# Gates of a PEER layer: tile 0's scattered by indirect DMAs into a table in HBM, tile 1's by one-hot products

## What is computed

```python
q = (xc @ wq).astype(F32).reshape(tc, H, 2, PEER_HALF)
s = jnp.einsum('thpd,hpnd->thpn', q, subkeys.astype(F32))
sv, si = lax.top_k(s, K)
cand = (sv[:, :, 0, :, None] + sv[:, :, 1, None, :]).reshape(tc, H, K * K)
cidx = (si[:, :, 0, :, None] * NK + si[:, :, 1, None, :]).reshape(tc, H, K * K)
best, pos = lax.top_k(cand, K)
eidx = jnp.take_along_axis(cidx, pos, axis=-1)
gates = jax.nn.softmax(best, axis=-1)
act = jax.nn.gelu(jnp.einsum('td,thkd->thk', xc, u_tab[eidx]).astype(F32), approximate=False)
w = (gates * act).astype(xc.dtype)
return jnp.einsum('thk,thkd->td', w, v_tab[eidx])
```

## Time and profile before

| what | value |
|---|---|
| median of 3 runs | 1063.74 us (1062.57 to 1065.11) |
| profiled execution | 1063.1 us |
| its span, first to last instruction | 1061.4 us |
| PE busy | 1039.0 us, 98% |
| DVE / ACT / POOL busy | 718.4 / 520.2 / 326.6 us |
| TensorE's granted clock, mean | 0.99 of full speed |
| moved by DMA | 205.43 MB, 194 GB/s on average |
| U's pieces of 512 KB | landing 3.7 us after issue |

### The profile page before, as it was taken

How to read it: one execution, slowest core, us unless ns; L and a number is a source line. 1 busy time by engine, 2 the same in 40 slices (tenths; PEclk the granted TensorE clock), 3 DMA queues, 4 the chain that set the end, 5 groups by cost and what they waited for, 6 DMA issues and landing times.

```text
span 1061.4 us, 18274 instructions
## 1 busy us (share of the span) xinstructions
PE 1039.0 (98%) x7154; PEld 963.8 (91%) x7154; DVE 718.4 (68%) x1601; ACT 520.2 (49%) x797; POOL 326.6 (31%) x161
## 2 busy tenths in 40 slices
PE   8999999889999999999999999999999999999996
PEld 8999889889999999999999999988888888888875
DVE  7778887964897069556666767765555756666556
ACT  5686657335444454544434343355544555455542
POOL 1000000001888788866666666600001000000002
PEclk9999999988999999999999999999999999999999
DMA  9878748544555555544444444456669567776651
GB/s 360 325 242 307 246 139 314 165 137 160 179 176 180 177 175 182 187 158 137 143 140 140 139 140 140 140 177 193 193 192 334 180 205 250 235 240 205 195 174 42
DMA packets 57413, 205.43 MB, mean 194 GB/s; under 512 B 6768, under 2 KB 8816, under 8 KB 56560
## 3 DMA queue, kind: packets, MB, share of 16 engines
q1 hardware_dynamic: 55616, 199.01, 57.0%
q0 software_dynamic: 1424, 5.24, 1.3%
q10 hardware_dynamic: 288, 0.01, 0.0%
HBM read 202.15 MB, written 2.10 MB: 192 GB/s over the span
## 4 chain that ended last, share of the span: by engine, by line
PE 91%; DVE 4%; ACT 1%; issue 1%; DMA 1%; SPq 0%; ACTq 0%; DVEq 0%
PE px L1079 33%; PE pw L786 16%; PE pw L787 16%; PE pw L788 15%; PE px L1051 5%; DMA ada<-in_ada 1%; DVE w_lo L1130 1%; PE px L1017 1%; PE px L786 1%; PE px L787 0%; PE px L788 0%; PE px L850 0%; ACT w_hi L487 0%; PE px L947 0%; PE pw L1099 0%
## 5 line engine op out<-in xcount | busy, mean ns | idle before, releaser
L487 ACT ACTIVATE w_hi<-raw 128x1024 fp32r<-128x1024 f32 x312 | 328.5, 1056 | 334.0 <-PE px L1079 168.8
L786 PE MATMUL pw<-a_hi,w_hi 128*128 128x256 f32 x1280 | 370.0, 289 | 2.1 <-DVE a_lo L1391 2.1
L787 PE MATMUL pw<-a_lo,w_hi 128*128 128x256 f32 x1280 | 362.6, 283 | 0.0
L788 PE MATMUL pw<-a_hi,w_lo 128*128 128x256 f32 x1280 | 362.5, 283 | 0.0
L420 POOL TENSOR_TENSOR w_lo<-raw,w_hi 128x1024 fp32r<-128x1024 f32 x128 | 307.5, 2403 | 142.2 <-ACT w_hi L487 140.9
L1130 DVE TENSOR_TENSOR w_lo<-raw,w_hi 128x1024 fp32r<-128x1024 f32 x184 | 224.5, 1229 | 156.0 <-ACT w_hi L487 155.3
L786 PEld LDWEIGHTS pw<-a_hi,w_hi 128*128 128x128 f32 x1280 | 245.8, 192 | 3.8 <-DVE a_lo L1391 2.5
L787 PEld LDWEIGHTS pw<-a_lo,w_hi 128*128 128x128 f32 x1280 | 246.1, 192 | 0.1
L788 PEld LDWEIGHTS pw<-a_hi,w_lo 128*128 128x128 f32 x1280 | 245.8, 192 | 0.0
L1079 PE MATMUL px<-w_hi,ws_hi 128*128 128x512 f32 x512 | 159.3, 390 | 0.9 <-DVE ws_lo L1543 0.9
L1079 PE MATMUL px<-w_lo,ws_hi 128*128 128x512 f32 x512 | 159.0, 389 | 0.0
(11 more groups left out here) (328 smaller groups left out, 1118.0 us busy)
## 6 DMA issues: line engine op xcount, KB each, us to landing
raw<-in_u SPq DMA_DIRECT2D x128, 512.0 KB, 3.7
raw<-in_v SPq DMA_DIRECT2D x128, 512.0 KB, 4.6
raw<-in_ws SPq DMA_DIRECT2D x56, 512.0 KB, 4.9
ada<-in_w_ada SPq DMA_DIRECT2D x32, 512.0 KB, 7.1
ada<-in_ada SPq DMA_DIRECT2D x6, 1024.0 KB, 11.1
raw<-in_w SPq DMA_DIRECT2D x7, 768.0 KB, 11.2
ada<-in_ada SPq DMA_DIRECT2D x4, 512.0 KB, 7.0
xT<-in_xT SPq DMA_DIRECT2D x8, 128.0 KB, 10.4
```

Source lines behind the costliest of these rows:

```text
L487: return nc.scalar.activation(out, in_, ACT.Copy, **kw)
L786: nc.tensor.matmul(out, lh, rh, start=start and x == 0, stop=False)
L787: nc.tensor.matmul(out, lh, rl, start=False, stop=False)
L788: last = nc.tensor.matmul(out, ll, rh, start=False, stop=stop and x == len(pairs) - 1)
```

## The change

Tile 0's gates no longer pass through one-hot products. A table of 128 x 128 x 128 floats in HBM (`gates_d`, 8.4 MB, laid out as j, i, token) is cleared, each gate of tile 0 is added into its place by indirect DMAs, and in V's stage each row's 64 KB are loaded back and multiplied into W's columns of tile 0. In detail:

- POOL clears the table by 8 DMAs of 1 MB from a zero tile of 256 floats per partition, one after every third of its splits. It now makes w_lo for U's first 26 pieces only, and DVE for the other 102.
- POOL then waits for the clears and for tile 0's gates, and issues 128 indirect DMAs (8 heads x 16 places), each with one word per partition and an add at its destination; before each further head it waits for all that it issued.
- DVE's top-k turns are cut into six steps. Tile 0's run in a row; tile 1's have a split before each step. `normal(0)` stands between the splits of U's pieces 27 and 28, and `normal(1)` at piece 74. The comparisons of both halves are one instruction each.
- The one-hot groups are 32, for tile 1's tokens from the last to the first, and come after the pieces 82 + 11n/8. iota is read from SBUF.
- SP waits, ahead of V's first piece, for the whole scatter and for the last one-hot matrices, then loads four rows of gates; from row 4 on, each load of V has one of gates behind it.
- DVE has a product `gate_w(r)` per V row, and ACT's `split_w` waits for it. ACT waits for the scatter at g = 63, since places and gates of tile 0 lie in W's last rows.

The diff, cut to its core:

```diff
-GA_U = 31
-OH = T // 4
-SCORES_AFTER = (4, 8, 11, 15)
-ENDS_AFTER = (18, GA_U - 2)
+SCORES_AFTER = (4, 8, 11, 14)
+POOL_PIECES = 26
+EXP_AFTER = (12, 36)
+NORMAL_AT = 74
+INDEX_AFTER = 38
+OH = P // 4
+OH_AT = [82 + 11 * n // 8 for n in range(OH)]
+GA_U = OH_AT[0] // 2
+ZERO = 256
+ZERO_DMAS = 8
...
+            def load_gates(r):
+
+                if r >= RING:
+                    sp.wait_ge(w_gated, r - RING + 1)
+                sp.dma_start(g_row[:, r % RING], gates_d[r * P * P:(r + 1) * P * P].rearrange("(i t) o -> i (t o)", i=P)) \
+                    .then_inc(g_landed[r % RING], 16)
+
             for m in range(UP, VP + NK):
+                if m == VP:
+                    sp.wait_ge(scattered, 16 * PH * TOPK)
+                    sp.wait_ge(oh_ready, OH)
+                    for r in range(RING):
+                        load_gates(r)
                 load_piece(m)
                 r = m - VP
+                if r >= RING:
+                    load_gates(r)
...
+            def clear(n):
+
+                pool.dma_start(table[n].rearrange("i (a f) -> i a f", f=ZERO),
+                               zero[:, :].unsqueeze(1).broadcast_to([P, NK * P // ZERO // ZERO_DMAS, ZERO])) \
+                    .then_inc(zero_landed, 16)
...
-            for m in range(UP, VP):
+            pool.wait_ge(zero_ready, 1)
+            for m in range(UP, UP + POOL_PIECES):
                 split_lo(m)
-
+                if (m - UP) % 3 == 2 and (m - UP) // 3 < ZERO_DMAS:
+                    clear((m - UP) // 3)
+
+            pool.wait_ge(zero_landed, 16 * ZERO_DMAS)
+            pool.wait_ge(gate_ready, 1)
+            for h in range(PH):
+                if h:
+                    pool.wait_ge(scattered, 16 * TOPK * h)
+                for k in range(TOPK):
+                    nc.gpsimd.indirect_dma_start(gates_d, bass.IndirectOffsetOnAxis(ap=place[:, h, k:k + 1], axis=0),
+                                                 gate[0][:, h, k:k + 1], None, compute_op=ALU.add).then_inc(scattered, 16)
...
             def split_w(v):
 
+                act.wait_ge(w_gated, v + 1)
...
+            for g in range(NG):
+                if g == 8:
+                    act.wait_ge(x1_spilled, 16)
                 if g == NG - 1:
-                    act.wait_ge(g_lower_taken, OH)
-                    for v in range(RING):
-                        split_w(v)
+                    act.wait_ge(scattered, 16 * PH * TOPK)
+                    for r in range(RING):
+                        split_w(r)
...
+            steps = (upper_half, lower_half, candidates, best_eight, next_eight, names)
...
+            for i in range(PH):
+                for step in steps:
+                    step(i)
+            gates(0)
+            upper_half(PH)
+            lower_half(PH)
+            dve.wait_ge(lo_ready, UP + POOL_PIECES)
+            m = UP + POOL_PIECES
+            for i in range(PH, TT * PH):
+                for n, step in enumerate(steps):
+                    split_lo(m)
+                    m += 1
+                    if i == PH and step is names:
+                        dve.wait_ge(zero_landed, 16 * ZERO_DMAS)
+                    if i > PH or n > 1:
+                        step(i)
+                    if i == PH and n == 1:
+                        normal(0)
+            gates(1)
+
+            def gate_w(r):
+
+                dve.wait_ge(g_landed[r % RING], 16 * (r // RING + 1))
+                dve.wait_ge(u_out, r // 2 + 1)
+                v.tensor_tensor(W[:, r, 0:P], W[:, r, 0:P], g_row[:, r % RING], ALU.mult).then_inc(w_gated, 1)
...
+            for p in range(m - UP - 3, 2 * NG):
+                split_lo(UP + p + 3)
+                if p == NORMAL_AT:
+                    normal(1)
+                if p == OH_AT[0] - 3:
+                    one_hots(0)
+                    one_hots(1)
+                if p in OH_AT:
+                    n = OH_AT.index(p)
                     take_lower(n)
                     if n + 2 < OH:
                         one_hots(n + 2)
-                if g == NG - 1:
+                if p == 2 * NG - 2:
+                    for r in range(RING):
+                        gate_w(r)
+                if p == 2 * NG - 1:
                     for r in range(RING):
                         split_w(r)
...
+                if p % 2 and p // 2 >= GA_U:
+                    gate_u(p // 2)
             split_lo(VP + 3)
+            gate_w(RING)
             for r in range(RING, NK):
+                if r + 1 < NK:
+                    gate_w(r + 1)
                 split_lo(VP + r)
                 split_w(r)
```

More of the change, by code:

```diff
@@ L119, in layer @@
         ones_pp = small("ones_pp", P)
+        token = small("token", 1)
         lb_raw = small("lb_raw", 2 * HG)
@@ L712, in _ @@
             split_hi(UP + 3)
[L715 to L738, removed]
-                     px[n % 4][:, :].rearrange("p (t j) -> p j t", t=4)[:, row:NK]).then_inc(g_upper_taken, 1)
             def split_w(v):
+                act.wait_ge(w_gated, v + 1)
                 if v >= RING:
@@ L763, in _ @@
-                if 2 * q < OH:
-                    take_upper(2 * q + 1)
+                left = T - 4 * taken(g)
+                last = nc.scalar.activation(W[:, 2 * g:2 * g + 2, 0:left], src[:, :, 0:left], ACT.Gelu)
+                if left < T:
+                    last = nc.scalar.activation(src[:, :, left:T], src[:, :, left:T], ACT.Gelu)
+                last.then_inc(u_out, 1)
+                split_hi(UP + 2 * g + 5)
+                if 2 * g + 1 in OH_AT:
+                    take_upper(OH_AT.index(2 * g + 1))
@@ L765, in _ @@
+                for t in range(TT):
+                    if g == EXP_AFTER[t]:
+                        act.wait_ge(best_ready, t + 1)
+                        nc.scalar.activation(gate[t][:, :], gate[t][:, :], ACT.Exp).then_inc(gate_exp, 1)
             for v in range(NK - RING):
-                if v + RING == 2 * GA_U:
-                    act.wait_ge(u_gated, NG - GA_U)
                 split_hi(VP + v + RING)
@@ new lines, in upper_half, with lower_half @@
+            def upper_half(i):
+                s = scored(i)
+                if i % 2 == 0:
+                    dve.wait_ge(score_done, i // 2 + 1)
+                at["first"] = [go(v.max(top_v[:, a, 0:8], s[a])) for a in range(2)]
+                need(at["first"][0])
+                v.max_index(top_i[:, 0, 0:8], top_v[:, 0, 0:8], s[0])
+                at["cut"] = go(v.match_replace(s_cut[:, 0], top_v[:, 0, 0:8], s[0], NEG))
+            def lower_half(i):
+                s = scored(i)
+                need(at["first"][1])
+                v.max_index(top_i[:, 1, 0:8], top_v[:, 1, 0:8], s[1])
+                v.match_replace(s_cut[:, 1], top_v[:, 1, 0:8], s[1], NEG).then_inc(score_used, 1)
+                need(at["cut"])
+                second = go(v.max(top_v[:, 0, 8:16], s_cut[:, 0]))
+                need(second)
+                v.max_index(top_i[:, 0, 8:16], top_v[:, 0, 8:16], s_cut[:, 0])
@@ L1484, in topk, with names @@
-                for a in range(2):
-                    need(key[a])
-                    last = go(v.tensor_reduce(ij[:, a, i], eq[:, a], AX, ALU.add))
-                return last
-            def gates(t, last):
-                q = slice(t * PH, (t + 1) * PH)
-                need(last)
-                v.tensor_tensor(gate[:, q], best[:, q], best[:, q, 0:1].broadcast_to([P, PH, TOPK]), ALU.subtract) \
+                at["places"] = go(v.tensor_copy(posf[:, :, :], pos2))
+            def names(i):
+                need(at["places"])
+                full = [P, 2, TOPK, TOPK]
+                hit = go(v.tensor_tensor(eq[:, :, :, :], posf[:, :, :].unsqueeze(3).broadcast_to(full),
+                                         iota16.unsqueeze(1).unsqueeze(1).broadcast_to(full), ALU.is_equal))
+                need(at["named"])
+                need(hit)
+                key = go(v.tensor_tensor(eq[:, :, :, :], eq[:, :, :, :], top_f.unsqueeze(2).broadcast_to(full), ALU.mult))
+                need(key)
+                at["last"] = go(v.tensor_reduce(ij[i // PH][:, :, i % PH], eq[:, :, :, :], AX, ALU.add))
@@ L1494, in gates @@
+            at = {}
+            steps = (upper_half, lower_half, candidates, best_eight, next_eight, names)
+            def gates(t):
+                need(at["last"])
+                v.tensor_tensor(gate[t][:, :, :], best[t][:, :, :], best[t][:, :, 0:1].broadcast_to([P, PH, TOPK]), ALU.subtract) \
                     .then_inc(best_ready, 1)
+                if t == 0:
+                    need(go(v.tensor_scalar(place_f[:, :, :], ij[0][:, 0], float(P), token[:, 0:1], ALU.mult, ALU.add)))
+                    v.scalar_tensor_tensor(place[:, :, :], ij[0][:, 1], float(P * P), place_f[:, :, :], ALU.mult, ALU.add)
```

193 lines of the change are left out of this document (80 added, 113 removed).

## The result

The changed kernel takes 1038.46 us, the median of 4 runs (1037.12 to 1039.74), against 1063.16 us for the kernel before (4 runs, 1062.57 to 1065.11). The ratio is 0.9764, with a 95% interval from 0.9743 to 0.9786: some 25 us faster. The profiled execution took 1039.74 us with a span of 1038.0, so it lies 1.3 us above its median.

The account below looks back on a forecast made before the run. PE, busy 98% of the span, was taken as the bound: 1063.1 - 28.7 (groups, transposes) + 1 (clears) + 1.2 (switch) + 0.8 (small stalls) = 1037.4, so 1038 us by the median; range 1033 to 1070.

Parts of the forecast that it names:

- The groups, -28.4: In U's stage, tile 0's 32 one-hot groups leave PE at 0.887 us each: 28.4 us less.
- DVE's splits hidden: In U's stage, DVE's splits stay behind PE's pace, with 15% to spare in tile 1's turns, 7% among one-hots.
- A clear's issue, 2.0: On POOL between U's splits, each 1 MB clear takes 2.0 us to issue against 1.9 hidden: 1 us in all.
- The issue of an indirect DMA, 1.2: On POOL, each scatter issue takes 1.2 us, twice a plain one; the scatter ends at 524 and costs 0.
- The limit of the forecast: At SP's wait ahead of V's first piece, the scatter has until 660 us, or 2.27 us for one issue.
- The switch, +1.2: Between U and V, PE waits 1.9 us where it waited 0.9 before: +1.2 us with the slack of signals.
- V's stage and small stalls, +0.8: V's gate loads and products are hidden; 0.8 us is added for small stalls at the exp and in V.
- (B): At SP's wait ahead of V's first load, the scatter comes late: slower, 128 x (issue - 2.27) us; chance 0.21.
- A: The forecast itself, 1034 to 1042 us, resting on the slack at each place; chance 0.55.
- (C): In U's stage, GpSimd's indirect issues hold DVE's splits back, 8 us and up to 14: 1046 to 1060; chance 0.12.
- (D): In U's stage, the clears hold POOL or the loads back, 5 to 21 us: 1042 to 1059; chance 0.08.
- (E): In the one-hot stretch, DVE's round trip replaces the removed groups, so nothing is won: 1061 to 1065; chance 0.04.

Follow-up runs that it names:

- the kernel with the earlier products: The changed kernel with DVE's gate products of V's first four rows one piece earlier, ahead of a split: 1035.94 us, and 1036.18 us when measured again.
- the buffers added: The kernel with the earlier products, plus a ring of seven rows of gates loaded three rows ahead of V's pieces: 1037.59 us, ratio 0.9756.

## Why the prediction was right, and where its terms were not

I forecast 1038.0 and the kernel took 1038.46. The mechanism was right: what PE no longer computes is what the end gains. By the traces the terms are -28.4 for the groups, -0.3 for the transposes (not measured by itself), 0 for the clears, +1.5 and +1.3, or -25.9 for the measured -25.7. That the sum comes as close as 0.5 us is partly luck, since its errors nearly cancel (the clears 1 us too much, the switch 0.3 and V with the small stalls 0.5 too little); and the largest error, in the scatter, cost nothing only because 3.3 us were left.

- **The groups, -28.4.** Right: 28.4 in U's stage with the groups alone taken out, and 32 of 0.89 in the chain of after.
- **DVE's splits hidden.** Right: w_lo waits for ACT's w_hi (143.6 us of its idle time), never the reverse, and PE waits for no w_lo in U's stage. DVE's w_lo behind the exp came in time too: DVE waited 7.0 us for ACT's gate, U's stage shows no loss by it (PE busy for 17.00 of the 17 us from 341 on).
- **A clear's issue, 2.0.** Mis-sized: 0.87. I had taken 1024 rows of 1 KB; the pages of the kernel without the scatter and of before count 3600 and 1424 packets for GpSimd's DMAs, so the eight clears went as 2176, of 3.9 KB each. The 1 us was 0. The DMA share was sized well (0.85 for 0.93), and it is the nearer limit: with the clears doubled the end came 5.8 us later.
- **The issue of an indirect DMA, 1.2.** This is the step that failed. I set it between the plain issue of 0.54 and 3.0 and chose "nearest to that row". It takes 1.55 at least, 1.77 on average, and 0.30 more to the next, a gap for which I had no term. A landing after each 16 took 3.3, not 2.2. The end came at 654 and not at 524. The limit of the forecast was good: 660 then, 657.5 in the trace.
- **The switch, +1.2.** Measured +1.5, by another count than mine. I took PE to wait 0.9 there before and 1.9 after. The 0.9 of before belongs to V's last products, at 1043.45, and stands in after as well. At the switch PE waited for nothing before, and 1.49 after. The 0.9 taken off was wrong, and the 1.9 was 0.4 too long, with 0.2 of slack on top: 0.9 one way and 0.6 the other.
- **V's stage and small stalls, +0.8.** Measured +1.3, and mostly in a place that I had no term for. 0.86 is GpSimd's closing DRAIN: 0.80 us before and with half the groups, 1.46 without the scatter, 1.66 with it, 1.99 and 2.64 with 132 and 140 indirect DMAs. So it grows with them, but 0.66 of the 0.86 is there without them, and what makes that part is not shown; the clears done twice leave it at 1.66. The other 0.45 lies in V's rows: 0.35 in the one stall behind a row of gates, which does not occur in the kernel with the earlier products, and 0.1 at V's first products.

On the rivals. (B), the late scatter, did not happen, but its place was right, and so was its kind of price: four more issues brought it about, and each further one costs its whole spacing, 1.85 us of V's start and 1.97 of the medians. I gave it 0.21; with the true size of the issue in hand it would have been a close call: 3.3 us over 128 are 0.026 us each, a little over 1% of the (226.9 + 48.1) / 128 = 2.15 from issue to issue, and 0.04 with the 2 us behind them. The chances are off by a hair: A, C and D alone add to 0.75, and I gave "faster" 0.74.

(C) had the right mechanism and the wrong victim. In after the issues at 396.30, 399.06 and 401.57 took 2.45, 2.21 and 2.15, and each started within a DVE split (396.11 to 397.33, 398.62 to 399.85, 401.07 to 402.30); the one at 404.03 started before the next split, at 404.37, and took 1.55, and that split took its 1.23. So the waiting is GpSimd's alone. The Trainium skill (SBUF — State Buffer, SBUF: two separate sides) says that the pair of ports is an exclusive lock, which whichever starts first holds against the other; for an issue that starts within a split the traces agree. For a split that starts within an issue they don't: the one at 404.37 was not held, and none of the 95 beside the scatter took more than 1.227 us. I had put DVE's loss at 8 to 14 us; it was none.

(D) and (E) did not occur: PE never waits beside the clears, and it is busy for all of the 299.2 us beside the scatter, in which nearly all of the one-hot stretch lies.

## What to carry to other kernels

A forecast that comes out is not yet understood: look how much of the cover that it relied on was left, and load the hidden resource until it shows. Price an indirect DMA of 128 single words at 2.1 us of GpSimd's time beside a busy DVE (1.77 and the gap of 0.30), not at twice a plain issue of 0.54 as I did, and compare the sum with the moment at which someone waits for the last. When work leaves the bound engine, read the switch between stages instruction by instruction: here four products moved ahead of one split were worth more than the buffers added.

## What the runs showed of the hardware that I had not expected

- An indirect DMA's issue that starts while DVE runs a split is lengthened by the rest of that split, from 1.55 to as much as 2.65 us, while the split keeps its 1.226. Twice, where a second split followed at once, the issue waited for that one too (2.80 and 2.77). A one-input tensor_scalar of 0.70 us did the same (1.95).
- GpSimd issues 1 MB of clears in 0.87 us, near the 0.76 of a plain load of 1 MB and the 0.54 of one of 512 KB. But with the DMA engines full (387 GB/s, share 1.01), the last clear was issued 8.9 us late, and with it came the split that PE needed.
- After PE had been idle for 6.7 us the granted clock was 0.50 in the next 6.0 us of full work, and after 21.6 us in the next 3.3. The idle 1.49 us of the switch left it at 1.00.
- GpSimd's closing DRAIN is not the same for every kernel: 0.80 us before, 1.66 after, 2.64 with 140 indirect DMAs, and in all of these runs the span ends 0.2 us after it.
